# Layer 0's modulation in column groups, with two thirds of it between the first groups of the input projection

## What is computed

```python
mods = split(silu(cond) @ w_ada[l] + b_ada[l], 6)      # cond: c for latents, c_ctx for context
sh1, sc1, gt1, sh2, sc2, gt2 = mods                    # 1024 values each
h  = rmsnorm(x, norm1_g[l]) * (1 + sc1) + sh1
x  = x + gt1 * mixer(h @ w_in[l]) @ w_out[l]           # w_in: 1024 x 2304; four kinds of attention or mixing
hh = rmsnorm(x, norm2_g[l]) * (1 + sc2) + sh2
x  = x + gt2 * (square(relu(hh @ w_mlp1[l])) @ w_mlp2[l])
```

## Time and profile before

| | |
|---|---|
| median of 3 runs | 4533.15 us (4532.97 to 4534.75) |
| the profiled execution | 4532.87 us, span 4531.5 us |
| mean granted TensorE clock | 0.96 |
| busy: PE, DVE, ACT, POOL | 91%, 46%, 20%, 13% |
| moved by DMA | 388.14 MB, mean 86 GB/s |
| first matmul of the input projection, layer 0 | 215.42 us |
| last barrier of that projection passed | 532.9 us |

### The profile page before, as it was taken

The page is one execution under the profiler, slowest core; times in us unless marked ns, Lnnn a source line. Parts: engine busy times, 40 slices in busy tenths (PEclk is TensorE's granted clock), DMA queues, the critical chain, the costliest instruction groups (busy, mean ns, idle before and its releaser), DMA issues.

```text
span 4531.5 us, 48956 instructions
## 1 busy us (share of the span) xinstructions
PE 4111.2 (91%) x19192; PEld 3109.5 (69%) x19192; DVE 2080.0 (46%) x3376; ACT 903.3 (20%) x1700; POOL 580.8 (13%) x484
## 2 busy tenths in 40 slices
PE   7589899889888999999967998997989899999998
PEld 2279655555566888888846885564648588888885
DVE  1222355545235666666634215554532554445444
ACT  0211155435011000000012114553510200000002
POOL 0111101100012111111102111110000211111112
PEclk9799899999999999999988998998999899999999
DMA  8333332564502211111222434246551011111111
GB/s 286 93 101 129 108 88 48 124 149 116 192 19 66 66 66 57 65 65 56 65 64 70 135 105 101 49 95 150 137 194 38 28 32 35 38 38 38 38 38 47
DMA packets 311683, 388.14 MB, mean 86 GB/s; under 512 B 107362, under 2 KB 225762, under 8 KB 311326
## 3 DMA queue, kind: packets, MB, share of 16 engines
q1 hardware_dynamic: 291038, 380.03, 28.7%
q10 hardware_dynamic: 20416, 4.98, 0.5%
HBM read 316.45 MB, written 73.47 MB: 86 GB/s over the span
## 4 chain that ended last, share of the span: by engine, by line
PE 82%; DMA 6%; DVE 4%; SPq 3%; POOL 2%; issue 2%; ACT 2%; ACTq 0%; POOLq 0%; DVEq 0%
PE bank L1677 19%; PE bank L1678 18%; PE bank L1679 18%; PE bank L1802 11%; PE bank L1754 3%; DMA s_den<-o_raw 2%; PE bank L685 2%; PE bank L1782 2%; PE bank L1842 2%; PE bank L1668 2%; POOL hf L724 1%; SPq L901 1%; DVE xT L1565 1%; PE bank L1856 1%; PE bank L1785 1%
## 5 line engine op out<-in xcount | busy, mean ns | idle before, releaser
L1677 PE MATMUL bank<-h_hi,w_hi 128*128 128x512 f32 (+1 forms) x2448 | 885.6, 362 | 62.4 <-DVE h_lo L700 61.5
L1678 PE MATMUL bank<-h_lo,w_hi 128*128 128x512 f32 (+1 forms) x2448 | 871.7, 356 | 0.0
L1679 PE MATMUL bank<-h_hi,w_lo 128*128 128x512 f32 (+1 forms) x2448 | 871.0, 356 | 0.0
L1565 DVE SCALAR_TENSOR_TENSOR xT<-bank,mods,xT 128x512 f32<-128x512 f32 (+1 forms) x816 | 536.8, 661 | 397.4 <-PE bank L1679 379.7
L1802 PE MATMUL bank<-prob,vv 128*128 128x512 f32 (+3 forms) x1504 | 710.9, 554 | 0.0
L1677 PE MATMUL bank<-m_hi,w_hi 128*128 128x512 f32 (+1 forms) x1536 | 568.3, 370 | 60.2 <-DVE xT L1565 52.5
L1677 PEld LDWEIGHTS bank<-h_hi,w_hi 128*128 128x128 f32 x2448 | 465.6, 190 | 137.4 <-DVE h_lo L700 66.5
L1678 PE MATMUL bank<-m_lo,w_hi 128*128 128x512 f32 (+1 forms) x1536 | 546.7, 356 | 0.0
L1679 PE MATMUL bank<-m_hi,w_lo 128*128 128x512 f32 (+1 forms) x1536 | 546.2, 356 | 0.0
L1678 PEld LDWEIGHTS bank<-h_lo,w_hi 128*128 128x128 f32 x2448 | 465.6, 190 | 70.8 <-issue 6.2
L1679 PEld LDWEIGHTS bank<-h_hi,w_lo 128*128 128x128 f32 x2448 | 465.4, 190 | 65.7
(11 more groups left out here) (140 smaller groups left out, 4676.8 us busy)
## 6 DMA issues: line engine op xcount, KB each, us to landing
stage<-in_w_mlp SPq DMA_DIRECT2D x64, 1024.0 KB, 5.3
ada_w<-in_w_ada SPq DMA_DIRECT2D x12, 2048.0 KB
nx_w<-in_w_ada SPq DMA_DIRECT2D x16, 1536.0 KB, 7.1
stage<-in_w_in SPq DMA_DIRECT2D x18, 1024.0 KB, 5.9
dft_t<-in_k_dft_lat SPq DMA_DIRECT2D x32, 512.0 KB, 5.9
rope_t<-in_k_rope SPq DMA_DIRECT2D x28, 512.0 KB, 4.0
k<-s_kB SPq DMA_DIRECT2D x48, 224.0 KB
k<-s_kA SPq DMA_DIRECT2D x24, 448.0 KB, 10.5
```

Source lines behind the costliest of these rows:

```text
L1565: dve.scalar_tensor_tensor(out=x, in0=bank[:, bk, :n], scalar=mods[l][:, gate + k, cd:cd + 1], in1=x, op0=ALU.mult, op1=ALU.add).then_inc( ...
L1677: x = pe.matmul(out, a_hi, b_hi, start=first, stop=False)
L1678: pe.matmul(out, a_hi, b_lo, start=False, stop=False)
L1679: return x, pe.matmul(out, a_lo, b_hi, start=False, stop=last)
```

## The change

- The sums of squares, roots and the first two reciprocals of norm 1 in layer 0 are done between the transposes of x, which start with each token block's arrival and use two banks instead of four.
- Only parts 0 to 3 of w_ada (sh1 and sc1) are made before norm 1. Part 4 follows group 4, parts 5 to 11 stand ahead of groups 8 to 14. They are loaded in halves of 1 MB into two tiles that lie in the third weight slot, so unit 2 is split only when they are used up.
- The matmuls of a part go to partitions 32 (k % 4) and the next one of bank 2, 3 or 7: four partial rows, which `columns` adds with a larger `pair` (K = 101, the bias in row 100). DVE clears two banks and part of m_row first.
- The barrier behind the modulation is gone. Three constants, the fills of s_toe and all table expansions come later; layer 1's expansions are in layer 1's projection.
- The cache groups are evacuated between the slices of the norm (after slices 1, 3, 5, 7 of block 0 and slice 1 of block 1); the loads and splits of units 2, 3 and 4 get later places.
- mods and mod_a are made in two steps, the second after group 24 (the sixth of unit 2), and POOL waits for it ahead of norm 2.

```diff
+BIAS_ROW = 100
+NADA, NADA1 = 12, 4
-    c["pair"] = np.array([[1, 0], [0, 1], [1, 1]], np.float32)
+    pair = (i[:, None] % 32 == np.arange(2)[None, :]).astype(np.float32)
+    pair[BIAS_ROW] = 1.0
...
+U_GROUPS = [[g["i"] for g in GROUPS if g["unit"] == u] for u in range(NU_IN)]
+LOAD_AT = [{U_GROUPS[u][0]: u + 2 for u in range(NU_IN - 2)} for _ in range(DEPTH)]
+LO_AT = [{U_GROUPS[u][3]: u + 2 for u in range(NU_IN - 2)} for _ in range(DEPTH)]
+for _t, _u, _at in ((LOAD_AT, 3, U_GROUPS[1][4]), (LOAD_AT, 4, U_GROUPS[2][2]), (LO_AT, 2, U_GROUPS[1][3]),
+                    (LO_AT, 3, U_GROUPS[2][1]), (LO_AT, 4, U_GROUPS[2][7])):
...
+ADA_AT = {U_GROUPS[0][0] + n - 4: n for n in range(NADA1 + 1, NADA)}
...
+    ada_h = [at(f"ada_h{i}", [P, KT // 2, 512], F32, W0 + 32768 + 8192 * i)[0] for i in range(2)]
...
     SP:
+        def load_ada_half(n, x):
+            if n > NADA1:
+                sp.wait_ge(half_used[x], n - NADA1)
+            sp.dma_start(ada_h[x], w_ada_v[0, :, x * (KT // 2):(x + 1) * (KT // 2), n * 512:(n + 1) * 512]
+                         ).then_inc(half_in[x], 16)
+            if x == 0:
+                sp.wait_ge(ada_cols, n - 3)
+                load_bias_row(n, half_in[0])
...
             load_unit(sp, l, 0, w_in_v[l, :, :, 0:UW])
+            if l == 0:
+                sp.wait_ge(xt_full, FT)
+                sp.wait_ge(cond_d, 3)
+                load_ada_half(NADA1, 0)
+                load_ada_half(NADA1, 1)
             load_unit(sp, l, 1, w_in_v[l, :, :, UW:2 * UW])
...
+                if g["i"] in LOAD_AT[l]:
+                    u = LOAD_AT[l][g["i"]]
                     load_unit(sp, l, u, w_in_v[l, :, :, u * UW:(u + 1) * UW])
+                if l == 0 and g["i"] in ADA_AT:
+                    load_ada_half(ADA_AT[g["i"]], 0)
+                    load_ada_half(ADA_AT[g["i"]], 1)
...
     POOL:
-        barrier(pool, 1)
         for l in range(DEPTH):
+            if l == 0:
+                pool.wait_ge(xt_full, FT)
             hi_unit(pool, l, 0, 0, None)
             hi_unit(pool, l, 1, 1, None)
-            pool.wait_ge(mod_rdy, l * 4 + 4)
+            pool.wait_ge(mod_rdy, l * 4 + 2)
...
+                    if l == 0 and u == 2:
+                        pool.wait_ge(half_used[1], NADA - NADA1)
...
     ACT:
+        def copy_rows(n):
+            if n < NADA1:
+                act.wait_ge(ada_rows, n + 1)
+            else:
+                act.wait_ge(half_used[1], n - NADA1 + 1)
+                act.wait_ge(ada_cols, n - 3)
+            act.activation(m_row[0:98, n % 4], bank[0:98, 2 + n % 2 if n < NADA1 else 7, :], ACT.Copy).then_inc(ada_copied, 1)
...
+        for i in range(FT):
+            c, k = divmod(i, KT)
+            if c and k == 4:
+                root(act, 0, c - 1)
+            act.wait_ge(xt_free, i + 1)
+            square_at(act, 0, c, k, k)
+        for n in range(NADA1):
+            copy_rows(n)
+        for l in range(DEPTH):
+            for h in range(0, 4):
+                act.dma_start(s_toe[l, h].rearrange("r c x -> (r c) x"), I["k_neg"]).then_inc(toe_neg, 16)
...
+            if l == 0:
+                for c in range(NCH):
+                    for k in range(KT):
+                        upper_norm(act, 0, c, k)
+                        if c * KT + k < 10 and k % 2:
+                            evacuate(GROUPS[(c * KT + k) // 2])
+                    if c == 0:
+                        root(act, 0, 2)
+                        copy_rows(NADA1)
...
             for g in GROUPS[5:]:
                 evacuate(g)
+                if l == 0 and g["i"] - 1 in ADA_AT:
+                    copy_rows(ADA_AT[g["i"] - 1])
+                x = g["i"] - U_GROUPS[1][2]
+                if x == 0:
+                    act.wait_ge(toe_neg, DEPTH * 4 * 16)
+                if 0 <= x < len(first):
+                    expand(*first[x])
...
     DVE:
+        inverse_root(dve, 0, 0)
+        inverse_root(dve, 0, 1)
+        lo_unit(dve, 0, 0, 0)
+        dve.wait_ge(ada_cols, NADA1)
...
+            if l == 0:
+                for c in range(NCH):
+                    if c == 2:
+                        inverse_root(dve, 0, c)
+                    for k in range(KT):
+                        scaled(dve, 0, c, k)
+                        if k:
+                            lower_norm(dve, 0, c, k - 1)
+                        if c * KT + k < 10 and k % 2:
+                            evacuate(GROUPS[(c * KT + k) // 2])
+                    lower_norm(dve, 0, c, KT - 1)
+                    if c == 0:
+                        lo_unit(dve, l, 1, 1)
...
     PE:
+            if i >= 3:
+                sum_square(pe, 0, *divmod(i - 3, KT))
...
+        def cond_rows(n, k, bk, w):
+            g = 32 * (k % 4)
+            return pe.matmul(bank[g:g + 2, bk], cond[:, k], w, start=(k < 4), stop=(k >= 4))
...
+        def ada_late(n):
+            if n > NADA1:
+                columns(n - 1)
+            else:
+                pe.wait_ge(n_std, NCH + CREDIT)
+            for x in range(2):
+                pe.wait_ge(half_in[x], (n - NADA1 + 1) * (32 if x == 0 else 16))
+                for k in range(KT // 2):
+                    mm = cond_rows(n, x * 4 + k, 7, ada_h[x][:, k])
+                mm.then_inc(half_used[x], 1)
...
             for g in GROUPS[:5]:
                 in_group(g)
+            if l == 0:
+                ada_late(NADA1)
+                pe.wait_ge(late_in, 3 * 16)
...
             for g in GROUPS[5:]:
+                if l == 0 and g["i"] - 2 in ADA_AT:
+                    ada_late(ADA_AT[g["i"] - 2])
+                if l == 0 and g["i"] == U_GROUPS[2][0]:
+                    columns(NADA - 1)
```

More of the change, by code:

```diff
@@ L757, in _ @@
-        barrier(sp, 1)
         for l in range(DEPTH):
@@ L1202, in evacuate @@
                     upper(p, zr[0])
[L1204 to L1206 removed]
+            if l == 0:
[8 more added lines that the diff above has]
+            else:
+                for g in GROUPS[:5]:
+                    evacuate(g)
+                norm_act(act, l * 2, lambda e, c: None)
             for g in GROUPS[5:]:
                 evacuate(g)
[L1209 to L1215 removed]
+                if l == 0 and g["i"] - 1 in ADA_AT:
[5 more added lines that the diff above has]
+                    expand(*first[x])
+                x -= len(first) + 8
+                if x == 0:
+                    act.wait_ge(toe_in, (l * TOE_DMAS + TOE_FIRST) * 16)
+                if 0 <= x < len(second):
+                    expand(*second[x])
+            barrier(act, l * PHASES + 1)
             act.wait_ge(lam_d, l * 5 + 2)
@@ L1378, in _, with scales @@
                 dve.wait_ge(ada_mods, 1)
-            for w in range(2):
+            def scales(w):
                 for cd in range(2):
@@ L1660, in columns @@
             for j in range(4):
                 x = (n * 4 + j) * 2
-                mm = pe.matmul(bank[:, 3, x:x + 2], m_row[0:3, n % 4, j * P:(j + 1) * P], pair, start=True, stop=True)
-            return mm
-        for n in range(12):
-            pe.wait_ge(ada_in[n % 4], (n // 4 + 1) * 32)
-            pe.wait_ge(ada_copied, n + 1)
+                mm = pe.matmul(bank[:, 1 if n < NADA1 else 6, x:x + 2], m_row[0:BIAS_ROW + 1, n % 4, j * P:(j + 1) * P],
+                               pair[0:BIAS_ROW + 1], start=True, stop=True)
@@ L1667, in _ @@
+            mm.then_inc(ada_cols, 1)
+        for n in range(NADA1):
+            pe.wait_ge(ada_in[n], 32)
+            if n >= 2:
+                pe.wait_ge(ada_copied, n - 1)
             for k in range(KT):
-                mm = pe.matmul(bank[0:2, n % 2, :], cond[:, k], ada_w[n % 4][:, k], start=(k == 0), stop=(k == KT - 1))
+                mm = cond_rows(n, k, 2 + n % 2, ada_w[n][:, k])
             mm.then_inc(ada_rows, 1)
             if n:
-                columns(n - 1).then_inc(ada_used, 1)
@@ L1672, in _ @@
-        columns(11).then_inc(ada_modp, 1)
-        barrier(pe, 1)
+                columns(n - 1)
+        columns(NADA1 - 1)
+        def ada_late(n):
+            if n > NADA1:
+                columns(n - 1)
+            else:
+                pe.wait_ge(n_std, NCH + CREDIT)
+            for x in range(2):
+                pe.wait_ge(half_in[x], (n - NADA1 + 1) * (32 if x == 0 else 16))
+                for k in range(KT // 2):
+                    mm = cond_rows(n, x * 4 + k, 7, ada_h[x][:, k])
+                mm.then_inc(half_used[x], 1)
```

223 lines of the change are left out of this document (137 added, 86 removed).

## The result

The changed kernel takes **4435.6 us** (median of 4 runs, 4426.8 to 4439.41) against 4533.95 for the kernel before, run beside it on the same chip: a ratio of 0.9779 (95% interval 0.9762 to 0.9796), 98 us faster. The forecast was 4428 us, 105 faster. The profiled execution took 4433.48 us with a span of 4432.2; before, 4532.87 and 4531.5, so 99.3 us between the two spans.

The account below looks back on a forecast made before the run. TensorE was taken as the bound, so the gain is the earlier start of group 14: 283 - 176 = 107, less 2 = 105 us; 4533 - 105 = 4428 us, range 4408 to 4470.

Parts of the forecast that it names:

- Loads: Start of the kernel: x lands from about 15 us to 23, four parts of w_ada by 46.
- Transposes and sums: Before norm 1: transposes alternate with sums of squares, 32 us from 15 to 47, under the loading of w_ada.
- rival B: Modulation: all four column groups overlap, 2.7 us a part, norm at 71, 4425 us; shares the forecast's 62%.
- Rival A: Modulation: column groups don't run side by side, 7.94 us a part, group 14 at 209, 4461 us; 28%.
- step 3: Four modulation parts before the norm: matmuls overlap by pairs, 3.9 us a part; ready at 67 us.
- Norm: Norm of token block 0: 4.65 us per two slices with a cache group, 20 us, ready at 88 against 215.
- Block 1: Norm of token block 1: ready at 106 us; part 4 and groups 5 and 6 hidden meanwhile.
- Late parts: Seven parts between groups 7 and 14: waits for loads before groups 9, 10 and 11; group 14 at 176 us.
- Rival C: Late parts: SP's queue paces them, loads at 12 us instead of 8.5, 25 us more, 4453 us; 7%.
- step 4: Before the norm: unit 1 converted at 67.5, norm starts at 68, first cache load lands with unit 1, fill costs nothing.
- step 8: Remaining columns, table expansions on ACT and lambda products: 2 us in all, the expansions costing nothing.

Follow-up runs that it names:

- experiment 7: Changed kernel with first weights and first cache tile loaded earlier, block 1's root behind all squares, fill spread over groups 21 to 28: 4426.27 us, ratio 0.9761.
- experiment 1: Changed kernel with all matmuls of a modulation part in one column group: 4468.74 us, ratio 0.9866.
- Experiments 2 and 3: Changed kernel with the s_toe fill at the head of ACT's program (4435.43 us), or behind group 15 with table expansions from group 23 (4431.82 us).
- experiment 3: Changed kernel with the s_toe fill issued behind group 15 and the table expansions from group 23: 4431.82 us, ratio 0.9789.
- after: The changed kernel itself, run beside the kernel before: 4435.6 us, ratio 0.9779.
- kernel 8: As experiment 7, with late parts ahead of groups 7, 9, 11 to 15 and part 6's load right behind part 5's: 4406.7 us, ratio 0.9722.

## Why the prediction was right, and where it was off

The forecast was 4428 us by a gain of 107 at group 14 less 2. Measured were 102.4 at group 14 and 98 at the end, inside the range and on the forecast's mechanism. By the steps:

1. *Loads:* x at 15 us; it was 11.5. The constants left in front take less than I gave them.
2. *Transposes and sums,* done at 47; 47.7. This is right by two errors that cancel: the start was 3.5 us early, and the last sums, of block 2, wait 4.86 us for a square that stands on ACT behind block 1's root, which waits 4.82 us for DVE's reciprocal of block 0. I had not followed that queue. With the root moved behind the squares (experiment 7) the wait is gone, but the norm, which waits for unit 1, starts no earlier.
3. *Four parts:* 3.9 us each by pairs; 1.90. **Mis-sized term.** All four groups overlap (rival B's case): 16 records go by fours, not by the pairs that I took for all that could run together. The modulation was ready at 59.6, not 67. Rival A fell with it; experiment 1 is rival A made real. Its 4468.74 us stands beside the 4461 that I gave for it, and its group 14 at 220.6 beside 209: rival A, too, had nothing for the fill, which holds the norm for 8.74 us there.
4. *What else the norm waits for:* unit 1 converted at 67.5; 65.8. But the fill "beside unit 1 and the cache", of which I wrote "I take none" with a bound of 3.5 us, is the **failed step**. It left ACT at 57.2 instead of 65, because step 3 was faster, and lay beside the first cache load, 256 KB that took 16.6 us. I had written that this load "is right behind unit 1 and lands with it". It came at 74, some 8 us behind unit 1, and a late cache group holds the norm, since DVE evacuates it ahead of the third slice. Experiments 2 and 3 measure the same 8 to 11 us elsewhere. It was not the earlier moment that made it dear: in experiment 1 the fill leaves ACT at 78 us and holds the next cache load for 13.94 us instead. The step priced the fill against unit 1 alone, "nearly in by then", and not against the chain of five cache loads behind it, each of which the norm waits for. The bound was wrong as well: by an even share 3.5 us, measured against the kernel with no fill there 9.7 us (cache group at 74.16 instead of 64.44). What step 3 gained, this took away: token block 0 was ready at 92 instead of 88. Rival B had the fill meet unit 1 and the norm start at 71; it started at 65.8 and then stood for 10.16 us.
5. *Norm:* 4.65 us for two slices; 4.98 (82.45 to 87.43 in GpSimd's timeline). A miss of 1.3 us in all.
6. *Block 1:* ready at 106; 110.9, of which 4 us are block 0's. Part 4 took 3.59 us and not 1.90, for TensorE came out of a nearly idle stretch: the granted clock from 90 to 94 us was 0.50. Hidden, as I had it.
7. *Late parts:* waits ahead of groups 9, 10 and 11 and no others over 0.4 us, as written. From group 7's start to group 14's I had 69.4 us (112 less 5.44 to 176); it took 69.7. That is two misses that cancel. A part takes 2.85 us instead of 4.88, 14 us less for seven. Against it the waits came to 8.0 us where mine were 2.5, the groups, taken as before (247.27 to 282.98), are 35.7 where I had 33, and some 6 us went at the lower clock level behind the waits, for which I had no term. Rival C (12 us for each load) would show waits ahead of all seven parts; three had them.
8. *Rest:* 2 us; 1.1 between group 14 and the projection's end. The expansions on ACT cost nothing that shows.

Of the 6.6 us between 105 forecast and 98.4 measured, 4.6 are there at group 14, from step 4's late cache load by way of steps 5 and 6. The other 2 are what was lost behind it beyond step 8's allowance, in the Fourier mixing, which the change doesn't touch. So the total came close partly by luck: step 3's gain and step 4's loss offset each other. The fall of rival A, which had made the range wide, is what the runs settle best.

*Page and trace, step 3.* The matmuls of a part went from 7.03 us to 1.90, 3.7 times, with four column groups and all rows of the array in use. The Trainium skill, "TensorE: Matmul & The Clock Gate", Part 3, gives 2.38 times for three column tiles and says that weight loads overlap a running matmul only where the row group differs. The measurement decides: here the four groups ran side by side without different rows, and their weight loads stand in the trace in fours, 0.10 us every 0.43, and lengthen nothing.

*Page and trace, step 4.* The cache load of 256 KB took 16.6 us beside the 3.84 MB from ACT's queue; with the fill elsewhere (experiment 3) it was issued at 58.66 us and used at 64.44, under 6 us. The Trainium skill's "Trainium Kernel Development and Optimization", Key Constraints, says that queues of several engines share the 16 DMA engines and interleave; the trace agrees, and I had weighed the rule and then not priced it. The delay was nearly three times what an even share gave.

## What to carry to other kernels

When a large transfer is moved, price it against everything that the other queues will issue while it runs, and not only against the one load that is there when it starts: behind that load may stand a chain of small ones, each waited for. Issued in one piece, the 3.84 MB cost 8 to 11 us in each of three places; in eight pieces, one per group, it cost nothing that shows. Deferred work that needs its own loads is best spaced so that the work between two pieces is longer than a load, since on TensorE a wait of a microsecond or two can be paid a second time in clock. And a change with several parts should be taken apart in runs: here the part that it is named for brought a quarter of the gain, and spreading the fill and spacing the late parts brought another 29 us. Taking apart goes for one's own mends too: of the three edits of experiment 7 one brought the gain.

## What the runs showed of the hardware that I had not expected

- Eight float32 matmuls (128 rows, 2 columns stationary, 512 moving) on four column groups take 1.90 us, on one 7.03. Coming from a nearly idle stretch, at a granted clock of 0.50, the same 16 records take 3.59.
- In after, waits of 1.2 to 2.7 us ahead of groups 9, 10 and 11 were each followed by 2 to 4 us of matmuls at the lower of the two clock levels (0.43 us apart instead of 0.23): about 6 us for 8 us of waits. With the waits gone the granted clock of that stretch was 1.00 instead of 0.83. It is not so each time: in kernel 7 waits of 1.43 and 2.05 us (ahead of groups 10 and 11) were followed by none, at a granted clock of 1.00, and in kernel 8 one of 2.09 us was.
- Beside the fill, issued in one go from another queue, small transfers came late: a cache load of 256 KB took 16.6 or 13.94 us (under 6 without the fill), a store of 256 KB 17.42 us (beside a weight load too), unit 0's load of 1 MB 18.88 us instead of 6.27. The fill's own eight pieces of 480 KB had a median of 9.5 us from issue to landing in after.
